# One-level Strassen scheme for the first product of four feed-forwards, with the second product laid between its block products

## The reference

```
hn = rms_norm(h, ln_mlp[layer])                                   # layers 0, 1
h = h + jnp.square(jax.nn.relu(hn @ w_mlp1[layer])) @ w_mlp2[layer]
...
mod = c_act @ ada_w[layer] + ada_b[layer]                         # layers 2, 3
h = rms_norm_2(x, norm_mlp[layer]) * (1.0 + scale2) + shift2
x = x + gate2 * (jnp.square(jax.nn.relu(h @ mlp_w1[layer])) @ mlp_w2[layer])
```

## Time and profile before

| what | value |
|---|---|
| median of 3 runs | 2666.29 us (2665.3 to 2666.81) |
| profiled execution, span | 2664.3 us (first to last instruction; the page gives no other time for it) |
| instructions | 35686 |
| PE busy | 2627.4 us, 99% |
| PE weight loads busy | 2069.3 us, 78% |
| DVE busy | 1268.0 us, 48% |
| ACT busy | 806.2 us, 30% |
| POOL busy | 1944.8 us, 73% |
| DMA | 272.08 MB, mean 102 GB/s |

### The profile page before, as it was taken

The page is one execution under the profiler, slowest core; times in us unless marked ns, Lnnn a source line. Parts: engine busy times, 40 slices in busy tenths (PEclk is TensorE's granted clock), DMA queues, the critical chain, the costliest instruction groups (busy, mean ns, idle before and its releaser), DMA issues.

```text
span 2664.3 us, 35686 instructions
## 1 busy us (share of the span) xinstructions
PE 2627.4 (99%) x12468; PEld 2069.3 (78%) x12468; DVE 1268.0 (48%) x1836; ACT 806.2 (30%) x1396; POOL 1944.8 (73%) x2832
## 2 busy tenths in 40 slices
PE   9999999999999999999999999999999999999999
PEld 6777788888766678888877888888887666788887
DVE  4766454442476655445234477511223776612211
ACT  4454311002255542101122254300113776401101
POOL 5533599998665559999876866887886555688875
PEclk9999999999999999999999999999999999999999
DMA  5211275653222126566322322333333211233332
GB/s 147 64 48 40 81 223 177 184 175 102 79 63 61 58 87 194 178 191 188 103 88 71 91 63 60 88 103 95 100 90 87 64 56 56 64 111 95 95 95 71
DMA packets 425151, 272.08 MB, mean 102 GB/s; under 512 B 9786, under 2 KB 411588, under 8 KB 425028
## 3 DMA queue, kind: packets, MB, share of 16 engines
q1 hardware_dynamic: 409154, 216.68, 28.1%
q10 hardware_dynamic: 15874, 53.67, 6.4%
HBM read 268.22 MB, written 2.10 MB: 101 GB/s over the span
## 4 chain that ended last, share of the span: by engine, by line
POOL 41%; PE 37%; issue 19%; DVE 1%; POOLq 1%; SPq 1%; DMA 0%; ACT 0%; DVEq 0%; ACTq 0%
POOL w_lo L400 28%; POOL w_hi L393 11%; PE ps L453 5%; PE ps L455 4%; PE ps L454 4%; PE pair L453 4%; PE pair L455 4%; PE pair L454 4%; POOL slot_mark L406 2%; PE ps L2041 2%; PE ps L2043 2%; PE ps L2042 2%; PE ps L1037 1%; PE pair L2451 1%; PE ps L1038 1%
## 5 line engine op out<-in xcount | busy, mean ns | idle before, releaser
L400 POOL TENSOR_TENSOR w_lo<-w_raw,w_hi 128x256 fp32r<-128x256 f32 x1612 | 1329.6, 856 | 33.6
L406 POOL TENSOR_TENSOR slot_mark<-slot_mark 128x1 f32<-128x1 f32 x400 | 98.9, 247 | 653.4 <-PE ps L455 346.8
L393 POOL TENSOR_SCALAR w_hi<-w_raw 128x512 fp32r<-128x512 f32 x806 | 533.6, 681 | 0.0
L453 PE MATMUL ps<-x_hi,w_hi 128*128 128x512 f32 x1040 | 423.5, 407 | 5.1 <-DVE x_lo L944 2.5
L455 PE MATMUL ps<-x_hi,w_lo 128*128 128x512 f32 x1040 | 406.1, 390 | 0.0
L454 PE MATMUL ps<-x_lo,w_hi 128*128 128x512 f32 x1040 | 405.3, 390 | 0.0
L1148 ACT ACTIVATE tt<-sq 128x512 f32<-128x512 f32 x128 | 81.1, 634 | 1029.5 <-DVE sq L1189 525.3
L453 PEld LDWEIGHTS ps<-x_hi,w_hi 128*128 128x128 f32 x1040 | 195.3, 188 | 52.6 <-issue 12.6
L454 PEld LDWEIGHTS ps<-x_lo,w_hi 128*128 128x128 f32 x1040 | 195.5, 188 | 42.5 <-issue 5.5
L455 PEld LDWEIGHTS ps<-x_hi,w_lo 128*128 128x128 f32 x1040 | 195.2, 188 | 42.0
L453 PE MATMUL pair<-x_hi,w_hi 128*128 128x512 f32 x544 | 212.2, 390 | 0.0
(11 more groups left out here) (442 smaller groups left out, 4396.0 us busy)
## 6 DMA issues: line engine op xcount, KB each, us to landing
w_raw<-in_w_mlp_dram SPq DMA_DIRECT2D x128, 512.0 KB, 4.1
w_raw<-in_mlp_w_dram SPq DMA_DIRECT2D x128, 512.0 KB, 4.0
arena<-in_ada_w_dram ACTq DMA_DIRECT2D x96, 512.0 KB, 4.0
w_raw<-in_w_in_ab_dram SPq DMA_DIRECT2D x28, 512.0 KB, 3.7
w_raw<-in_w_qkv_o_dram SPq DMA_DIRECT2D x24, 512.0 KB, 3.7
w_raw<-in_w_qkv_dram SPq DMA_DIRECT2D x24, 512.0 KB, 3.8
w_raw<-in_w_in_e_dram SPq DMA_DIRECT2D x23, 512.0 KB, 4.0
w_raw<-in_w_ple_gate_dram SPq DMA_DIRECT2D x16, 512.0 KB, 4.0
```

Of the source, the lines that this page charges most:

```text
L393: last = nc.gpsimd.tensor_scalar(w_hi[:, j, k, :], w_raw[:, j, k, :], 1.0, 1.0, ALU.mult, ALU.mult)
L400: last = nc.gpsimd.tensor_tensor(w_lo[:, j, k, :], w_raw[:, j, k, :], w_hi[:, j, k, :].bitcast(F32), ALU.subtract)
L406: nc.gpsimd.tensor_tensor(slot_mark[:, 0:1], slot_mark[:, 1:2], slot_mark[:, 1:2], ALU.subtract)
L453: nc.tensor.matmul(bank[:, :], w_hi[:, j, k, :], hi[:, k, :], start=(k == 0), stop=False)
```

## The change

The width 4096 is taken in sixteen steps of two chunks (`hp` 0 to 15; the second product takes two steps for each 512 rows of `w2`). The first six chunks of the first product are computed as before (`std`). The other 26 chunks form 13 pairs. A pair's weights are a block of 1024 x 256; rows are split in even and odd tiles, columns in the two chunks, and the tokens in two halves, and the product is formed from seven block products of half size in every dimension (Winograd's form): P1 to P7, each four tiles of k by three matmuls of 256 columns. The sums S1 to S4 of weights are made by DVE for each pair (`sums_13`, `sum_2`, `sum_4`), the sums T1 to T4 of the input once per feed-forward (`t_sums`, then cut by `t_high` on ACT and `t_low` on DVE into `xt_hi`, `xt_lo`). P1, P1 + P6 and P1 + P6 + P7 gather in one bank, and ACT copies each state out (`snap`); DVE adds the quarters (`first_quarter`, `last_quarters`, `second_quarter`) into `sq`.

The second product is cut in half chunks of four tiles of k ("g", 12 matmuls of 512 columns; four per `hp`), which are laid between the block products, and each is added to `h` at once (`add`): 64 adds per feed-forward for 32. Weights of pairs and g lie in eight half slots. POOL cuts the six standard chunks whole and the low parts of g; ACT makes the high parts of g and of all block products, DVE the low parts of the block products. Pair chunks are loaded into a ring of two `w_raw` slots and `raw_extra`, which lies in the arena where `t_tiles` (input for the sums T) lies before.

The ada products go to feed-forwards 0, 1 and 2, 32 each, beside pairs 1 to 12, with the sum over partitions after every 8. The loops of the feed-forwards are written out. Elsewhere some waits of set-up steps in the attention stages are replaced by `link`, the ple loads are issued by ACT at the end of the feed-forward instead of in the out-projection, and `at_dist` leaves the arena.

The diff's core:

```diff
+        arena_at[0] = 16 * T
+        t_tiles = take([ND, T])
+        arena_at[0] = 16 * T
+        raw_extra = take([ND, P])
...
+        PAIR = ["P1", "P2", "g0", "P4", "P5", "P6", "g1", "P7", "g2", "P3", "g3"]
...
+        SUM_OF = {"P7": "S3", "P5": "S1", "P6": "S2", "P3": "S4"}
...
+        RING = [4, 0, 1]
...
+        def pair_load(hp, which):
+            n = 2 * (hp - 1) + which
+            s = RING[n % 3]
+            return s, n // 3 + (0 if s == 4 else 2)
...
+            for hp in range(1, 14):
+                for which in range(2):
+                    n = 2 * (hp - 1) + which
+                    if n == 0:
+                        sp.wait_ge(*t_at(i, "lo3"))
+                    elif n < 3:
+                        sp.wait_ge(*std_cut(i, 3 + n))
+                    elif n % 2:
+                        sp.wait_ge(*low_cut(i, 1 + (n - 3) // 2, "S4"))
+                    else:
+                        sp.wait_ge(*low_cut(i, 1 + (n - 3) // 2, "P3"))
+                    chunk(pair_load(hp, which)[0], 4 * (hp // 2 + 1) + 2 * (hp % 2) + which)
+                for half in range(2):
+                    sp.wait_ge(*g_cut(i, hp - 1, 2 * half + 1))
+                    g_chunk(hp, half)
...
+                for c in range(4):
+                    n = place(hp, f"g{c}")
+                    pool.wait_ge(*high_cut(i, hp, f"g{c}"))
+                    for k in (slice(0, 2), slice(2, 4)):
+                        last = nc.gpsimd.tensor_tensor(half_slot(w_lo, n)[:, k, :], g_half(hp, c)[:, k, :],
+                                                       half_slot(w_hi, n)[:, k, :].bitcast(F32), ALU.subtract)
+                    last.then_inc(ml_pool, 1)
...
+        T3, T1, T4, T2 = (slice(HALF * n, HALF * (n + 1)) for n in range(4))
+        FIRST, SECOND = slice(0, HALF), slice(HALF, T)
+        first_sum, second_product, later_sums = ps[0], ps[1], ps[2]
...
+            def product(hp, what, out, b_hi, b_lo, start=True, stop=True):
+                n = place(hp, what)
+                pe.wait_ge(*low_cut(i, hp, what))
+                hi, lo = half_slot(w_hi, n), half_slot(w_lo, n)
+                for t in range(4):
+                    nc.tensor.matmul(out, hi[:, t, :], b_hi[:, t, :], start=(start and t == 0), stop=False,
+                                     skip_group_check=True)
+                    nc.tensor.matmul(out, hi[:, t, :], b_lo[:, t, :], start=False, stop=False, skip_group_check=True)
+                    last = nc.tensor.matmul(out, lo[:, t, :], b_hi[:, t, :], start=False, stop=(stop and t == 3),
+                                            skip_group_check=True)
+                last.then_inc(ml_spent, 1)
...
+            def g_product(hp, c):
+                n, e, bank = place(hp, f"g{c}"), hp // 2, g_bank(i, hp, c)
+                pe.wait_ge(*g_cut(i, hp, c))
+                if hp == 0 and c < 2:
+                    pe.wait_ge(*(norm_act.at(norm_before, "ln") if c else std_at(i, "free3")))
+                else:
+                    pe.wait_ge(*added(i, hp, c - 2))
...
-            for u, q, quarter in mlp_quarters(pe, i, True):
-                if i < 2:
-                    dense_pair(pe, (q, 0), (q, 1), *inner, normed(norm_before), wide=True, lag=3,
-                               within=(lambda: norm_tensor(pe, norm_before)) if isinstance(quarter, int) else None)
...
+            std(4, range(ND))
+            std(5, range(ND))
+            for c in range(4):
+                g_product(0, c)
...
+                    pe.wait_ge(*snapped(i, hp - 1, "P7"))
+                product(hp, "P1", first_sum[:, FIRST], *x_block(0, FIRST))
+                if hp == 1:
+                    pe.wait_ge(*std_at(i, "free5"))
+                else:
+                    pe.wait_ge(*pair_out(i, hp - 1, "C11"))
+                product(hp, "P2", second_product[:, FIRST], *x_block(1, FIRST))
+                g_product(hp, 0)
+                if hp == 1:
+                    pe.wait_ge(*t_at(i, "lo3"))
+                else:
+                    pe.wait_ge(*pair_out(i, hp - 1, "C12"))
+                product(hp, "P4", later_sums[:, FIRST], *t_block(T4))
+                product(hp, "P5", later_sums[:, SECOND], *t_block(T1))
+                pe.wait_ge(*snapped(i, hp, "P1"))
+                product(hp, "P6", first_sum[:, FIRST], *t_block(T2), start=False)
+                g_product(hp, 1)
+                pe.wait_ge(*snapped(i, hp, "P6"))
+                product(hp, "P7", first_sum[:, FIRST], *t_block(T3), start=False)
+                g_product(hp, 2)
+                pe.wait_ge(*pair_out(i, hp, "C2"))
+                product(hp, "P3", later_sums[:, SECOND], *x_block(1, SECOND), start=False)
...
+            def g_high(hp, c):
+                s, nth = g_load(hp, c // 2)
+                n = place(hp, f"g{c}")
+                act.wait_ge(*ml_loaded(i, s, nth))
+                act.wait_ge(*spent(i, n - 8))
+                nc.scalar.activation(half_slot(w_hi, n), g_half(hp, c), ACT.Copy).then_inc(ml_hi, 1)
...
+            def high(hp, what):
+                n = place(hp, what)
+                if what in SUM_OF:
+                    act.wait_ge(*low_cut(i, hp, SUM_OF[what]))
+                else:
+                    act.wait_ge(*ml_loaded(i, *pair_load(hp, int(what == "P4"))))
+                act.wait_ge(*spent(i, n - 8))
+                nc.scalar.activation(half_slot(w_hi, n), pair_block(hp, what), ACT.Copy).then_inc(ml_hi, 1)
+            def snap(hp, what, dst):
+                act.wait_ge(*spent(i, place(hp, what)))
+                if what == "P1" and hp > 1:
+                    act.wait_ge(*pair_out(i, hp - 1, "C12"))
+                nc.scalar.activation(dst, first_sum[:, FIRST], ACT.Copy).then_inc(ml_snap, 1)
...
+            for hp in range(1, 14):
...
+                high(hp, "P6")
+                snap(hp, "P1", snap_p1)
+                high(hp, "P7")
+                g_high(hp, 2)
+                ada_ahead(0)
+                high(hp, "P3")
+                g_high(hp, 3)
+                if hp < 13:
+                    high(ahead, "P1")
+                    high(ahead, "P2")
+                ada_ahead(1)
+                snap(hp, "P6", snap_q)
+                g_high(ahead, 0)
+                if hp < 13:
+                    high(ahead, "P4")
+                ada_ahead(2)
+                snap(hp, "P7", snap_v)
+                if hp < 13:
+                    high(ahead, "P5")
+                else:
+                    g_high(14, 1)
+                    g_high(14, 2)
+                pair_mid(hp, 1)
+                if hp < 13:
+                    g_high(ahead, 1)
+                else:
+                    g_high(14, 3)
+                pair_mid(hp, 0)
...
+            def t_sums(two):
+                def shift(k):
+                    return norm_gain(norm_before, k)[1]
...
+            def t_low(p):
+                v.wait_ge(*t_acted(i, "hi", p))
+                nc.vector.tensor_tensor(xt_lo[:, p, :], t_pair(p), xt_hi[:, p, :].bitcast(F32), ALU.subtract
+                                        ).then_inc(t_dve, 1)
+            def low(hp, what):
+                n = place(hp, what)
+                v.wait_ge(*high_cut(i, hp, what))
+                nc.vector.tensor_tensor(half_slot(w_lo, n), pair_block(hp, what), half_slot(w_hi, n).bitcast(F32),
+                                        ALU.subtract).then_inc(ml_low, 1)
+            def sums_13(hp):
+                a11, _ = quarters_of(hp, 0)
+                a21, a22 = quarters_of(hp, 1)
+                v.wait_ge(*ml_loaded(i, *pair_load(hp, 0)))
+                v.wait_ge(*ml_loaded(i, *pair_load(hp, 1)))
+                nc.vector.tensor_tensor(s3_tile, a11, a21, ALU.subtract).then_inc(ml_low, 1)
+                nc.vector.tensor_tensor(a21, a21, a22, ALU.add).then_inc(ml_low, 1)
...
+            def last_quarters(hp):
+                v.wait_ge(*spent(i, place(hp, "P7")))
+                v.wait_ge(*snapped(i, hp, "P7"))
+                v.wait_ge(*(pair_act(i, hp - 1, "sq1") if hp > 1 else std_acted(i, "sq", 5)))
+                nc.vector.tensor_tensor(sq[:, 1, :].rearrange("p (a t) -> p a t", a=2),
+                                        later_sums[:, :].rearrange("p (a t) -> p a t", a=2),
+                                        snap_v.unsqueeze(1).to_broadcast([P, 2, HALF]), ALU.add).then_inc(ml_out, 1)
...
+            def add(hp, c):
+                n = 4 * (hp % 2) + c
+                v.wait_ge(*spent(i, place(hp, f"g{c}")))
+                nc.vector.scalar_tensor_tensor(out=h[:, n, :], in0=g_bank(i, hp, c)[:, :], scalar=gate_col(layer2, 1, n),
+                                               in1=h[:, n, :], op0=ALU.mult, op1=ALU.add).then_inc(ml_added, 1)
...
+            std_out(0)
+            t_sums(0)
+            std_out(1)
+            std_rest(0)
+            t_low(0)
+            t_low(1)
+            std_rest(1)
+            std_out(2)
+            std_rest(2)
+            t_sums(1)
```

(91 more changed lines are left out.)

634 lines of the change are left out of this document (430 added, 204 removed).

## The result

The changed kernel takes 2675.87 us (median of 5, 2673.42 to 2676.9), the kernel before 2666.29 (2664.87 to 2666.81) beside it. The ratio is 1.0037, with a 95% interval of 1.0024 to 1.0049: slower, where 2636 us had been forecast. The profiled execution spans 2674.1 us, 9.8 more than before.

A forecast was written before the change was run, and what follows sets the result against it. PE was taken to bound the kernel. Products -55.2, start +20.6, loop +3 and `ada_sum` +1 gave -30.6 us on the profiled 2664.3, plus 2.0 outside that span: 2636 us; range 2608 to 2672, the forecast's own 2622 to 2652.

The forecast's parts named there:

- the start of a feed-forward: Uncovered chain delays g(0,2): 8.7 us each in feed-forwards 2 and 3, 1.6 in 0 and 1; +20.6 us, range 0 to 37.
- What bounds the kernel: PE, busy 2627.4 of 2664.3 us; relief of POOL, some 740 us of busy time, is worth nothing by itself.
- The products: Per feed-forward, 624 matmuls of 512 columns give way to 1092 of 256 at 0.1169 us; 55.2 us less for four.
- The sign that had been named: In the block products, a distance over 0.12 us between matmul starts would show the forecast wrong.
- Rival 3: Products: with full 128-column loads 256 columns take 0.125 to 0.13 us; 2671 us at 0.125, 2691 at 0.1295; chance 0.09.
- Boundaries at no cost: Between groups of PE matmuls, a boundary with satisfied waits costs nothing, read from two groups of 12 matmuls of 512 columns.
- The loop over pairs: PE's round takes 20.7 us and DVE's 18.5 hides beside it, so by the walk the loop costs PE nothing.
- The allowance of 3 us: Loop over pairs: 3 us added in all for pairs with three ada products, whose DVE round is some 0.5 longer.
- Rival 2: DVE's round exceeds PE's in feed-forwards 0 to 2, PE waiting at P3 on `last_quarters`; 2650 to 2748 us, chance 0.17.
- a microsecond or two for each long stall, in the range: Lower PE clock after the stalls at a feed-forward's start: that much on top of any case, left to the range.
- `ada_sum`: In the feed-forwards, 6 times 1.06 us become 12 of half the columns, about 0.6 each: +1 us.
- The end of each feed-forward: POOL cuts the next stage's chunks in time and DVE has room; nothing on either side beyond 1 us.

The follow-up runs named there:

- runs 4 and 5: Changed kernel's block-product matmuls: in 4 each split into two of 128 columns, 3130.18 us; in 5 only 64 of 128 weight columns used, 2656.1 us.
- run 3: Against the changed kernel: pair-chunk ring begins with w_raw slots 0 and 1, DVE and ACT work reordered at each feed-forward's start; 2639.11 us.

## Why the prediction was wrong, point by point

Two terms of the sum failed, by about 20 us each: the round of a pair (a matmul of 256 columns put at 0.1169 us, the boundary behind it at nothing) and the start of a feed-forward (20.6 us, with nothing for the lower clock). By the sum, either of them alone would have left the kernel some 10 us faster.

- **What bounds the kernel**: right. PE is the bound before and after; POOL's relief (1944.8 to 1323.4 us, 621 and not 740, as g's low parts took 957 ns in the mean instead of the 739 behind that figure) didn't help, since PE had not waited for POOL in such a stretch.
- **The products**: the step that failed is "I take 0.1169", read from matmuls with two weight columns. With 128 columns it is 0.1200: 4 x 1092 x 0.0031 = 13.5 us. The argument for it was that loads 0.11 apart are hidden behind the stream. It excluded only that load and stream add up; runs 4 and 5 show that a load nearly as long as the stream still costs some 4 ns (0.1200 against 0.116). The sign that had been named, a distance over 0.12, was set just too high to catch it. Rival 3 had the right cause and too large a size (0.125 to 0.13).
- **Boundaries at no cost**: wrong by 7 us. The earlier trace rows have 512 columns on both sides of the boundary; behind short ones the first five to nine matmuls of 512 columns are slow (0.14 us per round, 52 rounds). The trace of before has it too, behind most runs of short matmuls, for instance at the start of feed-forward 3 (timeline of PE there, first, seventh and tenth of 512 columns):

```profile
2305.66 0.40 PE L453 MATMUL ps<-x_hi,w_hi 128*128 128x512 f32 x1
2307.05 0.39 PE L453 MATMUL ps<-x_hi,w_hi 128*128 128x512 f32 x1
2307.73 0.59 PE L906 MATMUL pair<-rb,ones 128*128 128x512 f32 x1
```

  1.39 us for six, 0.232, then 0.68 for three, 0.227. I had looked at the 16 short ones and not behind them.
- **The loop over pairs**: right. DVE's round was put at 18.5 us and measures 245.65 / 13 = 18.9 in feed-forward 0; P3 waited for `last_quarters` once, 0.73 us in feed-forward 1. The allowance of 3 us was enough for waits. Rival 2 didn't come about. The upper end of the range, 2672, was put at a round of DVE of 21.6, but by the rival's own formula 21.6 gives 2659 and 2672 stands for 22.0; nothing here hangs on it.
- **The start of a feed-forward**: the mechanism and the place were right (chain, queue behind `low(1, "P1")`, g(0,2) waiting for `add`), the term of 20.6 us was mis-sized, it measures 41.5, more than the 37 named as its upper end. Of the difference 9.8 us are idle time: 5.2 and 4.6 us in feed-forwards 0 and 1 for 1.6, and 11.1 and 9.6 in 2 and 3 for 8.7. The walk had the last `t_low` of feed-forward 0 at 356.3 (about 359.1) and that of feed-forward 2 3 us early against PE's own start. The main reason is `t_sums`: in feed-forward 2 the two last 6.4 and 5.2 us and not some 4.3 and 3.5 as in the walk, with POOL in the way, as the rows below show for feed-forward 0. The other 11.1 us are 9.6 of the lower clock behind the stalls, which the sum left out ("a microsecond or two for each long stall, in the range"), and the 1.5 of the bars' overlap.

Timelines of POOL and DVE in feed-forward 0, `t_sums(1)`: two sums of 256 columns take 1.85 and 1.83 us while POOL cuts, and 0.75 and 0.74 once POOL is done at 354.35.

```profile
350.98 3.37 POOL L632 TENSOR_TENSOR w_lo<-w_raw,w_hi 128x256 fp32r<-128x256 f32 x4 [3.08 <-ACT w_hi L1457]
...
351.02 1.85 DVE L1601 TENSOR_TENSOR arena<-arena 128x256 f32<-128x256 f32 x2
352.80 1.83 DVE L1605 SCALAR_TENSOR_TENSOR arena<-arena 128x256 f32<-128x256 f32 x2
354.56 0.75 DVE L1610 SCALAR_TENSOR_TENSOR arena<-arena 128x256 f32<-128x256 f32 x2
355.23 0.74 DVE L1614 SCALAR_TENSOR_TENSOR arena<-arena 128x256 f32<-128x256 f32 x2
```

- **`ada_sum`**: +1.5 for +1. **The end of each feed-forward**: nothing beyond 1 us, as forecast.
- **The sum**: -30.6 forecast, +9.6 measured. The rounds are 20.4 us worse in all than at 20.7 each, of which 3 had been allowed; the start is 20.9 worse; some 2 are small terms. With the start mended (run 3) the kernel came to 2639 us, near the forecast 2636, but that is luck and not its sum: there the start costs some 4 us instead of 20.6, and the rounds 20 more.

## What to carry to other kernels

When a change halves the columns of a matmul, take its price from a row with the same weight columns, or bound it by the load; a row with narrow weights is a lower bound. When a new chain puts a wait into an engine's queue, list what stands behind the wait and needs nothing of it: moving two calls ahead of it gave back 28.7 of the 36.8 us, without shortening the chain. And the stalls on PE cost here about a third more than their length (9.6 us on 30.4), because the matmuls behind them ran at the lower clock.
